# Hybrid encoder layer on one core: LayerNorm ahead of the q/k sums, the root between two Gelu halves, the SSM output turned by channel halves, and the gated linear unit behind the first two scores of head 0

## The reference, cut to what matters

```
q = rms_norm(rms_norm(c_q) @ w_uq, q_norm)          # 8 heads of 96, then rotary
k = rms_norm([k_nope, k_pe], k_norm)                # needs sums of squares per token and head
y_attn = softmax(q k^T * scale + chunk mask) @ v    # block by block of 128 tokens

y = x_states @ C + d * u                            # SSM, 256 channels
z = gelu(y)
y_ssm = z * sigmoid(z @ w_glu)                      # the gated linear unit

y_conv = silu(layer_norm(depthwise_conv(...), ln_w, ln_b))   # 256 channels
```

## Time and profile before

| | |
|---|---|
| median of 3 runs | 1249.93 us |
| the profiled execution's own time | 1250.21 us |
| its span, first to last instruction | 1248.1 us |
| PE busy | 1129.5 us (90%) |
| DVE busy | 973.6 us (78%) |
| ACT busy | 702.0 us (56%) |
| POOL busy | 386.2 us (31%) |
| mean granted TensorE clock | 0.962 of full speed |

### The profile page before, as it was taken

The page is one execution under the profiler, slowest core; times in us unless marked ns, Lnnn a source line. Parts: engine busy times, 40 slices in busy tenths (PEclk is TensorE's granted clock), DMA queues, the critical chain, the costliest instruction groups (busy, mean ns, idle before and its releaser), DMA issues.

```text
span 1248.1 us, 15928 instructions
## 1 busy us (share of the span) xinstructions
PE 1129.5 (90%) x5636; PEld 865.2 (69%) x5636; DVE 973.6 (78%) x1182; ACT 702.0 (56%) x820; POOL 386.2 (31%) x359
## 2 busy tenths in 40 slices
PE   5979999888888889995799999999999999999992
PEld 3447564656566567885688888888887887787771
DVE  1999996756655745277799999999998999899971
ACT  5711225654445552223477777777777777777751
POOL 2340006287853000011222323333333332233220
PEclk8989989999999999996799999999999999999996
DMA  6700010000005010327599999999999999999930
GB/s 197 172 1 1 0 20 9 2 1 1 1 1 236 1 35 2 150 102 304 227 377 378 370 386 378 386 398 381 381 377 378 370 370 376 371 356 370 360 127 10
DMA packets 55484, 260.93 MB, mean 209 GB/s; under 512 B 31088, under 2 KB 31760, under 8 KB 41616
## 3 DMA queue, kind: packets, MB, share of 16 engines
q1 hardware_dynamic: 45344, 243.03, 50.7%
q0 software_dynamic: 10096, 17.34, 5.8%
HBM read 252.25 MB, written 26.35 MB: 223 GB/s over the span
## 4 chain that ended last, share of the span: by engine, by line
PE 70%; DVE 11%; DMA 8%; issue 4%; ACT 3%; SPq 2%; POOL 1%; DVEq 0%; ACTq 0%; POOLq 0%
PE psum L2118 27%; PE psum L2138 12%; DMA w<-in_w 7%; PE psum L2030 7%; PE psum L1763 3%; DVE arena L1112 3%; PE psum L1978 3%; PE psum L1801 3%; PE psum L1948 2%; PE psum L2108 2%; PE psum L1966 2%; PE psum L1841 1%; DVE am L1440 1%; DVE arena L1115 1%; PE psum L1934 1%
## 5 line engine op out<-in xcount | busy, mean ns | idle before, releaser
L1607 DVE TENSOR_TENSOR w_rest<-w,w_high 128x2048 fp32r<-128x2048 f32 x136 | 305.3, 2286 | 18.8 <-ACT w_high L1033 18.6
L1033 ACT ACTIVATE w_high<-w 128x2048 fp32r<-128x2048 f32 x136 | 256.3, 1912 | 72.1 <-DMA w<-in_w 51.8
L2118 PE MATMUL psum<-w_high,xgT_high 128*128 128x512 f32 x544 | 217.9, 400 | 11.4 <-DVE xgT_rest L1653 11.4
L2118 PE MATMUL psum<-w_rest,xgT_high 128*128 128x512 f32 x544 | 213.7, 393 | 0.0
L2118 PE MATMUL psum<-w_high,xgT_rest 128*128 128x512 f32 x544 | 212.9, 391 | 0.0
L1660 DVE TENSOR_TENSOR w_rest<-w,w_high 128x2048 fp32r<-128x2048 f32 x68 | 152.5, 2283 | 1.8 <-ACT w_high L1043 1.8
L1043 ACT ACTIVATE w_high<-w 128x2048 fp32r<-128x2048 f32 x68 | 126.3, 1907 | 19.7 <-DMA w<-in_w 19.6
L2118 PEld LDWEIGHTS psum<-w_high,xgT_high 128*128 128x128 f32 x544 | 102.9, 189 | 35.9 <-issue 13.0
L691 POOL DMA_INDIRECT out<-arena,idx x34 | 91.8, 2700 | 113.8 <-DVE arena L1673 110.6
L2118 PEld LDWEIGHTS psum<-w_rest,xgT_high 128*128 128x128 f32 x544 | 102.7, 189 | 22.5
L2118 PEld LDWEIGHTS psum<-w_high,xgT_rest 128*128 128x128 f32 x544 | 103.2, 190 | 20.4
(11 more groups left out here) (271 smaller groups left out, 2027.4 us busy)
## 6 DMA issues: line engine op xcount, KB each, us to landing
w<-in_w SPq DMA_DIRECT2D x102, 2048.0 KB, 18.5
arena<-in_x SPq DMA_DIRECT2D x5, 1024.0 KB, 5.0
h_scratch<-arena SPq DMA_DIRECT2D x8, 512.0 KB, 2.6
out<-arena SPq DMA_DIRECT2D x8, 512.0 KB, 3.6
arena<-in_x SPq DMA_DIRECT2D x1, 3072.0 KB, 19.1
arena<-in_w_in SPq DMA_DIRECT2D x1, 2688.0 KB, 13.8
arena<-in_w_in SPq DMA_DIRECT2D x1, 2048.0 KB, 12.1
wout_y_raw<-in_w_out SPq DMA_DIRECT2D x1, 2048.0 KB, 8.2
```

The costliest lines, as they stand in the source:

```text
L1033: act.activation(w13h[k][:, c, :], w13[b][k][:, c, :], ACT.Copy).then_inc(W13H_READY[k], 1)
L1607: dve.tensor_tensor(w13l[b][k][:, c, :], w13[b][k][:, c, :], w13h[k][:, c, :].bitcast(F32), S_).then_inc(W13_SPLIT[k], 1)
L2118: last = pe.matmul(psum[:, k, :], x_[:, c, :], w_[:, c, :], start=(c == 0 and n == 0), stop=(c == KC - 1 and n == 2))
```

## The change

Four edits, all in the stretch described above.

1. On GpSimd and VectorE the LayerNorm goes ahead of most of the q/k sums: GpSimd makes the reciprocal root after the squares of tile 1 (before: tile 3); VectorE takes the statistics before any sum, scales after tile 1, and puts weight and bias around tile 3; the sums of tiles 4 to 7 follow. TensorE turns the convolution after `project_qkv(0)` (before: after tile 2).
2. On ScalarE the Sqrt of the q/k mean squares stands between the two Gelu halves. The Sqrt of one column goes.
3. z is turned by channel halves through the ring banks (`F_Z`), each half as soon as its Gelu is done. Round `R_Z` goes.
4. The matmuls of the gated linear unit stand behind the scores of steps 0 and 1, and its Sigmoid stands behind the copies of head 0's keys and ahead of the Exp of step 0.

```diff
-        R_C, R_W, R_H, R_U, R_V, R_CONV, R_Y, R_Z, R_GLU = range(9)
+        R_C, R_W, R_H, R_U, R_V, R_CONV, R_Y, R_GLU = range(8)
+        F_Z = lambda c, b: F_QKV(NT - 1, 3) + 1 + 2 * c + b
...
-            for i in range(4):
+            for i in range(2):
                 square_qk(i)
             pool.wait_ge(ln_stats, 1)
...
-            for i in range(4, NT):
+            for i in range(2, NT):
                 square_qk(i)
...
-            save_z(0)
+            link(save_z(0))
+            act.sem_inc(z_ready, 1)
+            act.wait_ge(qk_mean, 1)
+            act.activation(at(14336 + 2816, 2 * NT * H), qks.rearrange("p a i h -> p (a i h)"), ACT.Sqrt).then_inc(qk_root, 1)
             link(save_z(1))
             act.sem_inc(z_ready, 1)
             act.sem_inc(hi_drained, 1)
-            act.activation(tmp[:, 0:1], ones[:, 0:1], ACT.Sqrt)
-            act.wait_ge(hi_filled, R_Z + 1)
-            for k in range(4):
-                last = act.activation(zT.rearrange("p c (k i j) -> p k i c j", k=4, i=2)[:, k],
-                                      psum[:, 4 + k, :].rearrange("p (i c j) -> p i c j", i=2, c=2), ACT.Copy)
-            last.then_inc(hi_drained, 1)
-            act.wait_ge(qk_mean, 1)
-            act.activation(at(14336 + 2816, 2 * NT * H), qks.rearrange("p a i h -> p (a i h)"), ACT.Sqrt).then_inc(qk_root, 1)
+            for c in range(2):
+                for b in range(2):
+                    act.wait_ge(lo_filled, F_Z(c, b) + 1)
+                    act.activation(zT[:, c, 512 * b:512 * (b + 1)], lo(F_Z(c, b)), ACT.Copy).then_inc(lo_drained, 1)
             act.wait_ge(ln_done, 1)
             act.activation(ctok, ctok, ACT.Silu).then_inc(conv_act_done, 1)
-            act.wait_ge(hi_filled, R_GLU + 1)
-            for k in range(4):
-                last = act.activation(sout[:, 2 * k:2 * k + 2, :], psum[:, 4 + k, :].rearrange("p (i n) -> p i n", i=2), ACT.Sigmoid)
-            link(last)
-            act.sem_inc(hi_drained, 1)
...
             for k in range(2):
                 save_kT(0, k)
+            act.wait_ge(hi_filled, R_GLU + 1)
+            for k in range(4):
+                last = act.activation(sout[:, 2 * k:2 * k + 2, :], psum[:, 4 + k, :].rearrange("p (i n) -> p i n", i=2), ACT.Sigmoid)
+            link(last)
+            act.sem_inc(hi_drained, 1)
             exponentials(0)
             exponentials(1)
...
-            for i in range(3):
-                project_qkv(i)
+            project_qkv(0)
             pe.wait_ge(conv_done, 1)
             turn(lambda i, c: cperm[:, c, i, :], R_CONV)
-            for i in range(3, NT):
+            for i in range(1, NT):
                 project_qkv(i)
...
-            pe.wait_ge(z_ready, 1)
-            turn(lambda i, c: yssm[:, i, c * P:(c + 1) * P], R_Z)
-            hi(R_GLU)
-            (32 rows of matmuls of the gated linear unit, unchanged)
+            for c in range(2):
+                pe.wait_ge(z_ready, c + 1)
+                for b in range(2):
+                    bank = lo(F_Z(c, b))
+                    for i in range(4):
+                        last = pe.transpose(bank[:, i * P:(i + 1) * P], yssm[:, 4 * b + i, c * P:(c + 1) * P], ident[:, :])
+                    last.then_inc(lo_filled, 1)
...
-                    pe.wait_ge(lo_drained, F_QKV(NT - 1, 3) + 1)
+                    pe.wait_ge(lo_drained, F_Z(1, 1) + 1)
...
             scores(0)
             scores(1)
+            hi(R_GLU)
+            pe.wait_ge(lo_drained, F_Z(1, 1) + 1)
+            (the matmuls of the gated linear unit)
             pe.wait_ge(hi_drained, R_GLU + 1)
             for n in range(STEPS):
```

More of the change, by code:

```diff
@@ L1363, in _ @@
             kp2 = at(14336 + 2560, NT, RD)
-            for i in range(2):
-                sum_qk(i)
             dve.wait_ge(hi_filled, R_CONV + 1)
@@ L1374, in _ @@
             dve.sem_inc(ln_stats, 1)
-            for i in range(2, 4):
+            for i in range(2):
                 sum_qk(i)
@@ L1381, in _ @@
             dve.sem_inc(hi_drained, 1)
-            for i in range(4, 6):
-                sum_qk(i)
+            sum_qk(2)
+            dve.wait_ge(row_par_in, 16 * 8)
+            tt(ctok, ctok, lnwb[:, 0, :].unsqueeze(1).to_broadcast([P, NT, CW]), M_)
+            sum_qk(3)
+            tt(ctok, ctok, lnwb[:, 1, :].unsqueeze(1).to_broadcast([P, NT, CW]), A_)
+            dve.sem_inc(ln_done, 1)
+            sum_qk(4)
             dve.wait_ge(scratch_in, 16)
@@ L1386, in _ @@
             link(dve.reduce_sum(st[:, 120:120 + NT], kp2, AX))
-            dve.wait_ge(row_par_in, 16 * 8)
             ts(qkw[:, 0, :], qkw[:, 0, :], SCALE, None, M_)
[L1389 to L1393, removed]
+            for i in range(5, NT):
+                sum_qk(i)
             tt(qks[:, 1], qks[:, 1], st[:, 120:120 + NT].unsqueeze(2).to_broadcast([P, NT, H]), A_)
@@ L1991, in _ @@
             scores(1)
+            hi(R_GLU)
+            pe.wait_ge(lo_drained, F_Z(1, 1) + 1)
+            for i in range(NT):
+                for c in range(2):
+                    last = pe.matmul(psum[:, 4 + i // 2, (i % 2) * 256:(i % 2 + 1) * 256], zT[:, c, i * P:(i + 1) * P], wglu[:, c, :],
+                                     start=(c == 0), stop=(c == 1))
+            last.then_inc(hi_filled, 1)
             pe.wait_ge(hi_drained, R_GLU + 1)
```

## The result

The changed kernel takes 1257.94 us, the median of 8 runs (1254.55 to 1264.39), against 1249.93 before (1248.9 to 1252.4): ratio 1.006, interval [1.004, 1.0081]. Run again as `a2_after_again` it took 1258.18, ratio 1.0065 [1.004, 1.0091]. It is slower by about 8 us; 1257.5 was forecast, +7.6.

What follows compares the result with a forecast made beforehand. TensorE, busy 90% of the span with 70% of the chain, was taken as the bound. Root gain −7.0, longer chain +10.65, clock falls +2.1 and +1.9 sum to +7.6: 1257.5 us, range 1252.5 to 1261.5.

Steps and rivals of the forecast that it cites:

- The 16 transposes in TensorE's idle time: Convolution's transposes fit into 3.06 us of idle time behind tile 0; everything after them on TensorE comes 1.75 us earlier.
- The root: Square root of q/k mean squares on ScalarE, ahead of head 0: there at 233.6 instead of 240.62, 7.0 us gained.
- The mean squares: q/k mean squares on VectorE, needed by 233.25 for the root: ready at 231.8, with 1.4 us to spare.
- The rival of the late root: Mean squares come at 235.84 as before, root 2.6 us later, time 1260.1; chance 0.07.
- The fixed chain: Head 0's transposes to first turned probabilities, through gated linear unit, Sigmoid and Exp: 18.2 us against 7.55, 10.65 lost.
- The falls: TensorE's clock drops to half after two idle gaps, before head 0's transposes and at the loop's start: 2.1 and 1.9 us.
- The lower end of the bracket for the second fall: Idle time behind the gated linear unit, 4.9 us, lies between 3.06 (no fall) and 7.3 (a fall).
- My sign of being wrong: First turned probabilities at 258 or earlier (263 to 264 forecast), or their difference not being the difference at the end.
- the shift survives the loop: In the attention loop the first turned probabilities' delay, 3.6 us before the clock's cost, stays to the end.
- Rival B: Theory weighed in the follow-up runs: the loss lies in the expert stage; no chance given.
- the rival of heads paced by GpSimd: Attention loop is paced by GpSimd's heads, which come 7.0 us earlier: time 1242.9; chance 0.05.
- The rival of a clock that holds: TensorE's clock stays full in one or both gaps: +3.6 to +5.5, 1253.5 to 1255.4 us; chance 0.20.

Runs made afterwards that it cites:

- e6: Kernel before with the first edit alone (LayerNorm ahead of the sums, convolution turned behind tile 0): 1247.48 us, ratio 0.9977.
- e1: Changed kernel with its fourth edit undone (gated linear unit ahead of head 0's transposes, Sigmoid ahead of head 0's keys): 1251.18 us, ratio 1.0007.
- e10: Changed kernel with matmuls that compute nothing (5, 13 and 20) filling TensorE's idle times around z and behind the gated linear unit: 1253.50 us, ratio 1.0011.
- e12: Changed kernel with 20, 47 and 40 transposes of the identity filling TensorE's idle times: 1252.59 us, ratio 1.0019.
- e4: Changed kernel with 20 transposes of the identity on TensorE behind the gated linear unit: 1256.82 us, ratio 1.0052.
- e2: Kernel before with the fourth edit alone (gated linear unit behind the scores, Sigmoid behind head 0's keys): 1269.31 us, ratio 1.0148.
- e3: Changed kernel with the Sigmoid behind the Exp of steps 0 and 1 instead of ahead of them: 1256.97 us, ratio 1.0051.
- e5: Changed kernel with 10, 24 and 20 transposes of the identity in TensorE's idle times around z and behind the gated linear unit: 1257.95 us, ratio 1.0048.
- e11: e9 plus 8 filler matmuls, 5 between the turns of z and 3 behind them: 1246.94 us, ratio 0.9975.
- e9: Changed kernel with the gated linear unit's matmuls back ahead of head 0's transposes, Sigmoid left behind the keys, no filler: 1250.76 us, ratio 1.0.

## Why the prediction was right, point by point

- The 16 transposes in TensorE's idle time: right. e6's SSM output ends 1.66 earlier, predicted 1.75. The 2.9 of the changed kernel's profile holds 1.1 that was there before the edit's place: tile 1's matmuls start at 193.68 and not at 194.79, as tile 0's and GpSimd's first roots ran that much earlier. In e1 and e6, which have the same edit, they start at 194.82 and 194.89, so the 1.1 is not the change's. (The SSM rotation ended at 196.36 on VectorE, not before 196; nothing hung on it.)
- The root: right. Predicted 0.7 after the end of the SSM output, measured 0.6 (232.37 against 231.77). The loads took 1.28 and no more: the Sqrt's from 230.75, the Sqrt at 232.05; the Exp's from 259.01, the Exp at 260.30. By the rule of the Trainium skill that was weighed (ScalarE: Activation LUTs, "What ACT_TABLE_LOAD costs"), each switch would have taken 1.4 longer; neither of the two does.
- The mean squares: right. Ready at 230.11, 1.9 us ahead of need; 1.4 predicted. The rival of the late root is out.
- The fixed chain: right within 0.2. From head 0's transposes to the first turned probabilities it is 18.0 us in e10 and e12, predicted 18.2. With the gain ahead of it, these two kernels have the first product with v 3.2 us later than before, once the different starts of tile 1 are taken out; predicted 3.6.
- The falls: both came, and both were sized a little high. The first was put at 2.1 and is 1.7 in the changed kernel's trace, the second at 1.9 and is 1.6 (4.87 against 3.29 from the first turned probabilities to the first product with v). So the terms of the sum come to +6.5 in the trace for a predicted +7.6.
- The median's +8.0 is nearer to the forecast than the terms are, and that is in part luck. The rest is no term of the sum: 1.2 to 1.4 near the loop's end, and 0.5 in the expert stage of the repeat. e4, with the same work up to the scores, had a first fall of 3.7 us, so the other executions of the changed kernel may hold such longer falls too; they have no trace, and how often that happens is open.
- The lower end of the bracket for the second fall was not firm: "3.06 (no fall)" held for one execution. In e2 the clock fell behind 3.10 us of idle time at the same place, in e6 at the end of 2.61 us and in e3 behind 2.20.
- My sign of being wrong was badly drawn. The first turned probabilities stand at 261.65, not at 263 to 264: 1.1 of that is the early start of tile 1, the rest the smaller fall and chain. And the difference there, +3.8, isn't the difference at the end, +7.3 in the repeat. The forecast itself put the second fall of 1.9 behind that row, so the two could not be the same.
- That the shift survives the loop: right. Rival B and the rival of heads paced by GpSimd are out; the loop got 2.8 longer, not shorter: 1.6 of it at its start, and 1.2 in the rest, where the clock was at half from 450.2 to 453.7 as well. Whether this late stretch belongs to the change is open: the late stretches differ from kernel to kernel, and e6, with the first edit alone, has three.
- The rival of a clock that holds: it had +3.6 to +5.5, where a hold in the second gap alone gives up to +5.75. With both gaps filled, e10 and e12 come to +1.4 and +2.4 us by their ratios, whose intervals reach to +3.8 and +4.4.

## What to carry to other kernels

Work that lies hidden under another engine is free only there. Before moving it, write down the chain that it would join at the new place, with the table loads and the in-order engines that it drags in: here 8.9 us that cost nothing became a chain 10.4 us longer, to gain 7 elsewhere. When a wait of TensorE gets longer, count the half clock behind it as a cost of its own, with a range, since the same program can have a short fall or a long one. If nothing useful fits, filler can hold the clock; here it paid where it filled the gap, and half of it brought nothing clear of the noise.

## What the runs showed of the hardware that was not expected

- One program's time goes with the clock it happened to be granted. The 35 runs of the kernel before in the third group lie between 1246.6 and 1257.7 us with mean granted clocks from 0.956 to 0.970; the correlation is −0.89 (−0.80 and −0.76 in the other two groups), and 0.01 of clock goes with 6.4 us. Three runs, as shown ahead of the prediction, hide this.
- How long the clock stays at half after work has begun again differs from execution to execution. Up to the scores the changed kernel, its repeat, e3 and e4 do the same work: behind head 0's first transpose the clock took 3.5, 3.5, 4.3 and 8.6 us to come back. In e2 it took 8.9, and in e5 it was at half over a window of 9.7 us of which 8.92 were busy.
- Filler on TensorE that computes nothing was worth 4.7 us in the traces up to the loop's end and 4.7 to 5.6 by the medians where it filled the gaps (e10, e12), 3.1 in e11 against e9, and at most 0.2% where it filled half (e4, e5).
